# Where a two-model transformer kernel keeps its split weights and its activation rows in SBUF

## The chip, the cores and the metric

One core of one Trainium2 chip. The metric is the device time of one execution in microseconds (us); the kernel before is given as the median of three runs, and one further execution was profiled.

## The reference

Two small transformer blocks follow each other, each with two layers, on one sequence of 256 tokens with 1024 features, in float32. Layer of the first block: feed-forward, a mixing stage (latent attention, a gated recurrence, attention over a memory), feed-forward. Layer of the second block: feed-forward, a mixing stage (an RWKV-7 scan, a retention group), feed-forward. Cut to what matters here:

```python
for l in range(2):
    x = x + 0.5 * swiglu(rmsnorm(x, ffn1_norm[l]), w_ffn1_in[l], w_ffn1_out[l])   # 1024 -> 2*2816 -> 1024
    u = rmsnorm(x, mix_norm[l])
    c_q, c_kv, k_r, hq, hf, hi, hgate, mq, gate_logits = split_sizes(u @ w_in[l], IN_SPLITS)
    ...
    x = x + merged @ w_out[l]
    x = x + 0.5 * swiglu(rmsnorm(x, ffn2_norm[l]), w_ffn2_in[l], w_ffn2_out[l])
```

Nearly all the arithmetic is products of a [256, K] activation with a [K, N] weight matrix that is used once.

## The kernel before, in words

Activations lie transposed: features on the 128 partitions, the 256 tokens in the free dimension, so that one 128-feature tile of `x` is a row of 256 floats (1024 bytes) in each partition. All weights come from HBM as one stream of 128x128 blocks in the order in which they are used.

**Products in three parts.** A float32 product is made of three TensorE matmuls in the rounded type float32r: the operands are split into a high part and the remainder, and `hi*hi`, `hi*lo` and `lo*hi` are added up in PSUM. `gemm` does it for one block: the stationary operand is the block's high part (slot `sb_whi`), with the activations' high row `xh` and then their low row `xl` moving; then the block's low part (slot `sb_wlo`) with `xh` moving. Each is a 128x128 stationary operand and a 256-column moving one. There are 17,628 such matmuls. In 312 more (`gemm_rows`) the roles are changed: 128 columns of the activations are stationary and 512 columns of the weights move. The attention, recurrence and scan parts use plain float32 matmuls of several sizes.

**The weight pipeline.** SP loads a chunk of 16 blocks (1 MB) into one of three `sb_raw` slots (`load_chunk`). A piece is 8 blocks: ScalarE (ACT) copies it, rounded, into one of four `sb_whi` slots (`split_hi`), VectorE (DVE) writes the remainder to the `sb_wlo` slot of the same number (`split_lo`), and TensorE (PE) reads both (`take`). A slot is written again when PE has used its piece. `split_ahead` issues the splits up to four pieces ahead.

**The placement.** `sbuf` takes tensors one after another from the low end. The large area of temporaries, `arena`, lies at the high end, and `area` places tiles in it at fixed offsets:

```python
ctx.enter_context(nc.sbuf_tensor("arena", [128, ARENA], F32, side="right"))
k.arena, k.placed = nc.sbuf_usable_end // 32 * 32 - 4 * ARENA, 0
k.xh, k.xl = (area(k, (XH + NX * i) * T, NX, T, dt=F32R) for i in range(2))
```

Addresses are byte offsets within a partition. In the program as built the four `sb_whi` slots begin at 56480, 60576, 64672 and 68768 and the four `sb_wlo` slots at 72864, 76960, 81056 and 85152: all are 160 past a multiple of 1024, that is 32 past a multiple of 64. A block is 512 bytes, so blocks begin 160 or 672 past a multiple of 1024. The `arena` begins at 90080, and every 1024-byte row in it begins 992 past a multiple of 1024, again 32 past a multiple of 64. Rows of `xh` and `xl`, which hold the normalized input of a stage, are the moving operand in 11,712 of the 17,628 matmuls; other rows of the arena (the hidden layer of the feed-forward, the outputs of the branches) in the other 5,916.

The order of the work is written out by the Python code itself: each engine has a list of instructions and explicit semaphore waits.

Of the kernel before, what the change touches and what calls it, by code (L numbers as in the profile page):

```python
# [11 lines left out]
F32 = mybir.dt.float32  # L12
F32R = mybir.dt.float32r
# [3 lines left out]
T = 256  # L17
D = 1024
NX = 8
# [4 lines left out]
PIECE = 8  # L24
CHUNK_BLOCKS = 16
PER_CHUNK = CHUNK_BLOCKS // PIECE
WARM = 7
RAW_SLOTS = 3
SPLIT_SLOTS = 4
AHEAD1 = (2, (6, 2))  # L30
AHEAD2 = (4, (1, 1, 1, 1))
# [193 lines left out]
STATE2 = 108 * T  # L225
XH = 120
assert STATE2 + NC2 <= XH * T
ARENA = (XH + 16) * T


def constants():
# [72 lines left out]
def activation(out, a, f, **kw):  # L304

    return lambda e: e.activation(out, a, f, **kw)  # L306
# [92 lines left out]
def new_slot(k, name):  # L399

    slot = State()
    slot.sem, slot.count = k.ctx.enter_context(k.nc.semaphore(name)), 0
    return slot


def sbuf(k, name, shape, dt=F32):
    return k.ctx.enter_context(k.nc.sbuf_tensor("sb_" + name, shape, dt))


def area(k, at, *shape, dt=F32, rows=128):  # L410

    n = int(np.prod(shape))
    assert dt == U8 or at + n <= ARENA, (at, n)
    k.placed += 1
    a = k.nc.alloc_sbuf_tensor_at(f"area{k.placed}", [rows, n], dt, offset=k.arena + 4 * at)[:, :]
    if len(shape) == 1:
        return a
    names = "abcd"[:len(shape)]
    return a.rearrange(f"p ({' '.join(names)}) -> p {' '.join(names)}", **dict(zip(names, shape)))
# [26 lines left out]

def start_weights(k, stream):

    w = k.w = State()
    w.stream, w.chunks, w.pieces, w.at = stream, stream.shape[0], stream.shape[0] * PER_CHUNK, 0
    w.raw = [sbuf(k, f"raw{i}", [128, CHUNK_BLOCKS * 128]) for i in range(RAW_SLOTS)]
    w.hi = [sbuf(k, f"whi{i}", [128, PIECE * 128], F32R) for i in range(SPLIT_SLOTS)]
    w.lo = [sbuf(k, f"wlo{i}", [128, PIECE * 128], F32R) for i in range(SPLIT_SLOTS)]
    w.slots = [new_slot(k, f"raw_in{i}") for i in range(RAW_SLOTS)]
    w.loaded, w.hi_done, w.lo_done, w.used = {}, {}, {}, {}


def load_chunk(k, c):  # L460
    w = k.w
    if c >= w.chunks:
        return
    if c >= RAW_SLOTS:
        k.sp.wait(k.dve, w.lo_done[(c - RAW_SLOTS + 1) * PER_CHUNK - 1])
    n = k.sp.dma(w.slots[c % RAW_SLOTS], w.raw[c % RAW_SLOTS][:, :], w.stream[c])
    for p in range(PER_CHUNK):
        w.loaded[c * PER_CHUNK + p] = (w.slots[c % RAW_SLOTS], n)

# [10 lines left out]
def raw_piece(k, n):  # L480
    c, part = divmod(n, PER_CHUNK)
    return k.w.raw[c % RAW_SLOTS][:, part * PIECE * 128:(part + 1) * PIECE * 128]


def split_hi(k, n):
    w = k.w
    k.act.wait(*w.loaded[n])
    if n >= SPLIT_SLOTS:
        k.act.wait(k.pe, w.used[n - SPLIT_SLOTS])
    w.hi_done[n] = k.act.mark(activation(w.hi[n % SPLIT_SLOTS][:, :], raw_piece(k, n), ACT.Copy))  # L490


def split_lo(k, n):
    w = k.w
    k.dve.wait(k.act, w.hi_done[n])
    if n >= SPLIT_SLOTS:
        k.dve.wait(k.pe, w.used[n - SPLIT_SLOTS])
# [163 lines left out]
def scales(k, name, at=None):  # L661


    sc = State()
    if at is None:
        sc.ssq, sc.diag, sc.sq = (sbuf(k, f"{name}_{n}", [128, T])[:, :] for n in ("ssq", "diag", "sq"))
        sc.ms, sc.tm = (sbuf(k, f"{name}_{n}", [128, 2])[:, :] for n in ("ms", "tm"))
    else:
        sc.ssq, sc.diag, sc.sq = (area(k, at + T * i, T) for i in range(3))
        sc.ms, sc.tm = area(k, at + 3 * T, 2), area(k, at + 3 * T + 8, 2)  # L670
    sc.rs = sc.diag
    return sc
# [1047 lines left out]
def prelude2(k):  # L1720

    k.act.wait(k.pe, k.pe.count)
    k.act.wait(k.dve, k.dve.count)
    k.c2 = area(k, STATE2, NC2)
    k.c2_slot = new_slot(k, "in_c2")
    k.c2_in = k.act.dma(k.c2_slot, k.c2, k.io["c2"])
    k.lora_slot = new_slot(k, "in_lora")
# [787 lines left out]
def gains(phases):  # L2515

    names = {"f1": "ffn1_norm", "mix": "mix_norm", "f2": "ffn2_norm"}
    out = []
    for i in reversed(range(len(phases))):
        p = phases[i]  # L2520
        s = "_2" if p[0] == "B" else ""
        out.append(("final_norm" + s, None, out[-1] if out else None) if p.endswith("norm") else
                   (names[p[2:]] + s, int(p[1])))
    return out[::-1]


def warm_up(k):


    zeros = area(k, (2 * NF + 9) * T, T)  # L2530
    k.pe.wait(k.dve, k.dve.mark(memset(zeros, 0.0)))
    for i in range(WARM):
        k.pe.mark(matmul(k.bank[7][:, 0:T], zeros[:, 0:128], zeros))
# [29 lines left out]
def constants_ready(k):  # L2563

    if k.constants:
        for q in (k.pe, k.act, k.dve, k.pool):
            q.wait(*k.constants)
        k.constants = None


def store(k):
    slot = new_slot(k, "stored")
    for j in range(0, NX, 2):
        k.sp.wait(k.dve, k.x_done[j + 1])
        n = k.sp.dma(slot, k.io["out"][:, j:j + 2, :], k.x[:, j:j + 2, :])
    k.sp.wait(slot, n)


def program(nc, io, phases=PHASES):
    with ExitStack() as ctx:  # L2580
        k = State()
        k.nc, k.ctx, k.io = nc, ctx, io
        k.later, k.fillers, k.unsettled, k.units, k.emptied = deque(), deque(), None, 0, {}
        k.two, k.preloaded = None, 0
        k.sp, k.pe, k.act, k.dve, k.pool = (Queue(ctx.enter_context(nc.semaphore(f"done_{n}")))
                                            for n in ("sp", "pe", "act", "dve", "pool"))
        k.bank = [ctx.enter_context(nc.psum_tensor(f"bank{i}", [128, 512], F32)) for i in range(8)]
        k.x, k.vecs, k.c1 = sbuf(k, "x", [128, NX, T]), sbuf(k, "vecs", [128, NV]), sbuf(k, "c1", [128, NC1])
        k.sx, k.scratch = scales(k, "x"), sbuf(k, "scratch", [128, 2])[:, :]
        ctx.enter_context(nc.sbuf_tensor("arena", [128, ARENA], F32, side="right"))  # L2590
        k.arena, k.placed = nc.sbuf_usable_end // 32 * 32 - 4 * ARENA, 0
        k.xh, k.xl = (area(k, (XH + NX * i) * T, NX, T, dt=F32R) for i in range(2))
        k.x_done, k.xh_done, k.xl_done = [0] * NX, [0] * NX, [0] * NX
        g = gains(phases) + [None]
        start_weights(k, io["stream"])
        if phases[0].endswith(("f1", "f2")):
            warm_up(k)
        start(k, g[0])
        steps = []
        if any(p in ("A0mix", "A1mix") for p in phases):  # L2600
            steps = prelude1(k)
            if not phases[0].endswith(("f1", "f2")):
                constants_ready(k)
            if phases[0] not in ("A0f1", "A0f2", "A1f1"):
                for step in steps:
                    step()
                steps = []
        for i, p in enumerate(phases):
            between = {}
            if p in ("A0f1", "A0f2", "A1f1") and steps:  # L2610
                between.update({1 + j: step for j, step in enumerate(steps)})
                steps = []
            if p in ("A0f1", "A1f1") and phases[i + 1:]:
                between[14] = lambda l=int(p[1]): memory_operands(k, l)
            if p == "B0f1" or (i == 0 and p in ("B0mix", "B0f2", "B1f1", "B1mix")):
                between[2] = lambda: prelude2(k)
            if p.endswith("norm"):
                if g[i + 1] is None:
                    final(k)
            elif p in ("A0mix", "A1mix"):  # L2620
                if i == 0:
                    memory_operands(k, int(p[1]))
                mix1(k, int(p[1]), g[i + 1])
            elif p in ("B0mix", "B1mix"):
                if i == 0:
                    prelude2(k)
                mix2(k, int(p[1]), g[i + 1])
            else:
                ffn(k, g[i + 1], between, lag=i == 0)
        store(k)  # L2630
        with nc.Block() as block:
            @block.sync
            def _(e):
                k.sp.replay(e)

            @block.tensor
            def _(e):
                k.pe.replay(e)

            @block.scalar  # L2640
            def _(e):
                k.act.replay(e)

            @block.vector
            def _(e):
                k.dve.replay(e)

            @block.gpsimd
            def _(e):
                k.pool.replay(e)  # L2650
# [34 lines left out]
```

How the kernel before makes its waits and increments, by code:

```python
    def wait(self, other, count):  # L375
        if count:
            self.todo.append(lambda e: e.wait_ge(other.sem, count))
# [4 lines left out]
    def mark(self, what):  # L383
        self.count += 1
        self.todo.append(lambda e: what(e).then_inc(self.sem, 1))
        return self.count
# [1 line left out]
    def dma(self, slot, out, a):  # L388
        slot.count += 16
        self.todo.append(lambda e: e.dma_start(out, a).then_inc(slot.sem, 16))
        return slot.count
```

## Time and profile before

| | |
|---|---|
| median of three runs | 2478.52 us (2473.41 to 2479.93) |
| the profiled execution, its own time | 2470.84 us |
| its span in the profile | 2469.0 us |
| TensorE busy | 2440.9 us, 99% of the span, 20,948 matmul records |
| mean granted TensorE clock | 0.996 |
| VectorE, ScalarE, GpSimd busy | 68%, 52%, 16% |
| moved from HBM | 405.89 MB, 165 GB/s over the span |

The span runs from the first to the last instruction of the profiled execution; 1.8 us of its time lie around it. Matmuls are pipelined, and their ends are modelled: the mean duration of a record (280 ns) overlaps the next ones, and it is the distance from one start to the next that tells what a matmul takes of the engine's time. Below, that distance is called the pace.

### The profile page before, as it was taken

The numbers are of one execution on the slowest core, as the hardware profiler recorded it, in microseconds if no ns is written. First come the engines' busy times: TensorE is split into PE (matmuls) and PEld (weight loads), VectorE is DVE, ScalarE is ACT, GpSimd is POOL, SyncE is SP. The second block draws the span as 40 slices with busy tenths as digits, with TensorE's granted clock in tenths as the row PEclk, the third lists the DMA queues.
The fourth block names the chain that finished last, engine by engine and source line by source line (L and its number), as shares of the span: only waits on it lengthen the run. The fifth ranks groups of instructions, "written<-read, shape, count | busy, mean of one in ns | idle before, by whom it ended". The sixth has DMA issues, their size and how long they took to land.

```text
span 2469.0 us, 49272 instructions
## 1 busy us (share of the span) xinstructions
PE 2440.9 (99%) x20948; PEld 2380.7 (96%) x20948; DVE 1673.3 (68%) x2315; ACT 1279.0 (52%) x1812; POOL 404.8 (16%) x357
## 2 busy tenths in 40 slices
PE   8999999999999999999999999999999999999998
PEld 8999999999999999999999999989999999999998
DVE  7765776866667657878666766866666665866664
ACT  5544656644445456565454544745444444754443
POOL 4012110300200210203003013512002003422001
PEclk9999999999999999999999999999999999999999
DMA  6555433455555544345555555403555555402553
GB/s 241 188 188 180 162 124 133 173 188 186 188 188 188 188 171 154 120 139 195 185 190 191 205 203 183 155 19 120 186 185 179 187 189 186 161 26 98 193 188 120
DMA packets 57675, 410.11 MB, mean 166 GB/s; under 512 B 6384, under 2 KB 6640, under 8 KB 8688
## 3 DMA queue, kind: packets, MB, share of 16 engines
q1 hardware_dynamic: 56592, 402.15, 45.9%
q10 hardware_dynamic: 864, 4.82, 0.5%
q8 instruction: 165, 2.70, 0.4%
q14 instruction: 54, 0.44, 0.1%
HBM read 405.89 MB, written 1.05 MB: 165 GB/s over the span
## 4 chain that ended last, share of the span: by engine, by line
PE 87%; DVE 5%; ACT 3%; issue 3%; POOL 2%; DMA 0%; DVEq 0%; SPq 0%; POOLq 0%; ACTq 0%
PE bank L297 86%; DVE sb_wlo L310 2%; ACT area L306 2%; DVE area L310 2%; DVE area L321 1%; PE bank L301 1%; ACT sb_whi L306 1%; POOL area L310 0%; ACT L306 0%; POOL sb_x_ssq L310 0%; POOL area L315 0%; POOL sb_x_sq L310 0%; DVE sb_x L321 0%; DMA sb_x<-x 0%; POOL area L334 0%
## 5 line engine op out<-in xcount | busy, mean ns | idle before, releaser
L297 PE MATMUL bank<-area,sb_whi 128*128 128x256 f32 x11752 | 2093.6, 281 | 11.0 <-DVE area L321 5.7
L297 PEld LDWEIGHTS bank<-area,sb_whi 128*128 128x128 f32 x11752 | 1799.7, 188 | 23.8 <-DVE area L321 9.6
L297 PE MATMUL bank<-area,sb_wlo 128*128 128x256 f32 x5876 | 1642.3, 279 | 4.5 <-DVE sb_wlo L310 4.4
L306 ACT ACTIVATE sb_whi<-sb_raw 128x1024 fp32r<-128x1024 f32 x762 | 801.9, 1058 | 777.0 <-PE bank L297 771.0
L297 PEld LDWEIGHTS bank<-area,sb_wlo 128*128 128x128 f32 x5876 | 1103.6, 188 | 6.4 <-DVE sb_wlo L310 6.4
L310 DVE TENSOR_TENSOR sb_wlo<-sb_raw,sb_whi 128x1024 fp32r<-128x1024 f32 x762 | 962.0, 1271 | 163.2 <-ACT sb_whi L306 161.8
L310 DVE TENSOR_TENSOR area<-area,area 128x256 f32<-128x256 f32 (+7 forms) x502 | 259.7, 526 | 248.4 <-ACT area L306 245.7
L306 ACT ACTIVATE area<-area 128x256 f32<-128x256 f32 (+6 forms) x515 | 252.1, 498 | 83.9 <-DVE area L310 59.1
L310 DVE TENSOR_TENSOR area<-bank,sb_x_diag 128x512 f32<-128x512 f32 x244 | 167.3, 686 | 36.2 <-PE bank L297 21.6
L297 PE MATMUL bank<-area,area 128*64 128x64 f32 (+5 forms) x2304 | 181.4, 254 | 2.1 <-ACT area L306 1.9
L310 POOL TENSOR_TENSOR sb_x_ssq<-sb_x 128x256 f32<-128x256 f32 x12 | 13.1, 1088 | 1014.9 <-DVE sb_x L321 883.0
L297 PEld LDWEIGHTS bank<-area,area 128*64 128x64 f32 (+2 forms) x2304 | 157.8, 157 | 21.2 <-ACT area L306 7.7
L306 ACT ACTIVATE area<-bank 64x512 f32<-64x512 f32 (+5 forms) x174 | 88.0, 514 | 153.1 <-PE bank L301 112.3
L310 DVE TENSOR_TENSOR area<-bank,area 128x512 f32<-128x512 f32 (+5 forms) x204 | 105.1, 543 | 81.3 <-PE bank L297 44.2
L310 POOL TENSOR_TENSOR sb_x_sq<-sb_x 128x256 f32<-128x256 f32 x84 | 102.0, 1214 | 232.4 <-DVE sb_x L321 228.9
L321 DVE SCALAR_TENSOR_TENSOR sb_x<-bank,sb_x 128x256 f32<-128x256 f32 x96 | 39.5, 422 | 138.6 <-PE bank L297 138.6
L310 POOL TENSOR_TENSOR area<-area 128x512 f32<-128x512 f32 (+1 forms) x66 | 73.3, 1111 | 352.6 <-DVE area L310 177.6
L306 ACT ACTIVATE area<-sb_x,sb_vecs 128x256 fp32r<-128x256 f32 (+1 forms) x96 | 47.0, 506 | 76.1 <-DVE sb_x L321 73.2
L310 POOL TENSOR_TENSOR sb_x_ssq<-sb_x_ssq,sb_x_sq 128x256 f32<-128x256 f32 x87 | 79.7, 916 | 26.3 <-ACT sb_x_sq L306 19.7
L321 DVE SCALAR_TENSOR_TENSOR area<-sb_x,sb_vecs,area 128x256 fp32r<-128x256 f32 x88 | 70.3, 814 | 10.1 <-ACT area L306 10.1
L310 POOL TENSOR_TENSOR area<-area,area 128x256 f32<-128x256 f32 (+2 forms) x36 | 53.8, 1507 | 93.4 <-ACT area L306 36.0
L297 PE MATMUL bank<-sb_whi,area 128*128 128x512 f32 x208 | 66.6, 401 | 1.0 <-ACT area L306 0.6
(82 smaller groups left out, 705.7 us busy)
## 6 DMA issues: line engine op xcount, KB each, us to landing
sb_raw<-stream SPq DMA_DIRECT2D x379, 1024.0 KB, 4.8
sb_raw<-stream SPq DMA_DIRECT2D x4, 512.0 KB, 6.9
area<-lora ACTq DMA_DIRECT2D x2, 768.0 KB, 4.5
area<-c ACTq DMA_DIRECT2D x1, 1504.0 KB, 7.2
sb_x<-x SPq DMA_DIRECT2D x4, 256.0 KB, 5.0
area<-mem ACTq DMA_DIRECT2D x1, 1024.0 KB, 8.2
out<-sb_x SPq DMA_DIRECT2D x4, 256.0 KB, 2.9
area<-m ACTq DMA_DIRECT2D x1, 512.0 KB, 5.8
```

Of the source, the lines that this page charges most:

```text
L297: return lambda e: e.matmul(out, lhsT, rhs, start=start, stop=stop, skip_group_check=True, tile_position=at)
L301: return lambda e: e.transpose(out, a, ident)
L306: return lambda e: e.activation(out, a, f, **kw)
L310: return lambda e: e.tensor_tensor(out, a, b, op)
L321: return lambda e: e.scalar_tensor_tensor(out, a, s, b, op0, op1)
```

## The change

No instruction is added, removed or moved: both programs have the same instructions in the same order on every engine, with the same waits. What differs is where tiles lie.

- A new function `place` puts the arena at a multiple of 1024 bytes, and below it, from the highest down, the weight slots: slot 3, then 2, 1 and 0, in each the high part above the low part, each tile 64 * (i + 1) past a multiple of 1024. Below them lie the three raw slots.
- The rows of `xh` and `xl` are moved up by 8 floats, so that they begin 32 past a multiple of 1024. All other rows of the arena begin at a multiple of 1024.
- The scratch for descriptors of dynamic DMAs, at the low end of SBUF, goes from 16384 to 1024 bytes, which makes room for the gaps.

In the program as built:

| tile | before, past a multiple of 1024 | after |
|---|---|---|
| `sb_whi` and `sb_wlo` slots 0, 1, 2, 3 | 160, 160, 160, 160 | 64, 128, 192, 256 |
| the odd blocks in them | 672 in all | 576, 640, 704, 768 |
| rows of `xh`, `xl` | 992 | 32 |
| other 1024-byte rows of the arena | 992 | 0 |
| `sb_raw` slots | 160 | 64 |
| `sb_x`, `sb_vecs` and the constants in `sb_c1` | 128, 128, 32 | 128, 128, 32 |

```diff
+ROW = 4 * T
...
-ARENA = (XH + 16) * T
+ARENA = (XH + 16) * T + 8
...
+def place(k, end):
+    k.arena = (end - 4 * ARENA) // ROW * ROW
+    at, k.split_at = k.arena, {}
+    for i in range(SPLIT_SLOTS)[::-1]:
+        for part in range(2):
+            rest = 64 * (i + 1)
+            at = (at - 4 * PIECE * 128 - rest) // ROW * ROW + rest
+            k.split_at[part, i] = at
+    k.raw_at = []
+    for i in range(RAW_SLOTS):
+        at -= 4 * CHUNK_BLOCKS * 128
+        k.raw_at.append(at // 32 * 32)
+    return k.raw_at[-1]
...
-    w.raw = [sbuf(k, f"raw{i}", [128, CHUNK_BLOCKS * 128]) for i in range(RAW_SLOTS)]
-    w.hi = [sbuf(k, f"whi{i}", [128, PIECE * 128], F32R) for i in range(SPLIT_SLOTS)]
-    w.lo = [sbuf(k, f"wlo{i}", [128, PIECE * 128], F32R) for i in range(SPLIT_SLOTS)]
+    nc, piece, chunk = k.nc, [128, PIECE * 128], [128, CHUNK_BLOCKS * 128]
+    w.hi, w.lo = ([nc.alloc_sbuf_tensor_at(f"sb_{name}{i}", piece, F32R, offset=k.split_at[part, i])
+                   for i in range(SPLIT_SLOTS)] for part, name in enumerate(("whi", "wlo")))
+    w.raw = [nc.alloc_sbuf_tensor_at(f"sb_raw{i}", chunk, F32, offset=k.raw_at[i]) for i in range(RAW_SLOTS)]
...
-        ctx.enter_context(nc.sbuf_tensor("arena", [128, ARENA], F32, side="right"))
-        k.arena, k.placed = nc.sbuf_usable_end // 32 * 32 - 4 * ARENA, 0
-        k.xh, k.xl = (area(k, (XH + NX * i) * T, NX, T, dt=F32R) for i in range(2))
+        k.placed = 0
+        low = place(k, nc.sbuf_usable_end // 32 * 32)
+        ctx.enter_context(nc.sbuf_tensor("placed", [128, (nc.sbuf_usable_end - low) // 32 * 8], F32, side="right"))
+        k.xh, k.xl = (area(k, (XH + NX * i) * T + 8, NX, T, dt=F32R) for i in range(2))
...
-    nc = bacc.Bacc("TRN2", target_bir_lowering=False, num_devices=1)
+    nc = bacc.Bacc("TRN2", target_bir_lowering=False, num_devices=1, dynamic_dma_scratch_size=1024)
```

## Rows read from the trace of the kernel before

**Rows 1.** The page, busy time and instructions of each engine.

```profile
PE 2440.9 (99%) x20948; PEld 2380.7 (96%) x20948; DVE 1673.3 (68%) x2315; ACT 1279.0 (52%) x1812; POOL 404.8 (16%) x357
```

**Rows 2.** The page, the chain that ended last, by engine.

```profile
PE 87%; DVE 5%; ACT 3%; issue 3%; POOL 2%; DMA 0%; DVEq 0%; SPq 0%; POOLq 0%; ACTq 0%
```

**Rows 3.** The page, groups of instructions: busy, mean ns; idle before, releaser.

```profile
L297 PE MATMUL bank<-area,sb_whi 128*128 128x256 f32 x11752 | 2093.6, 281 | 11.0 <-DVE area L321 5.7
L297 PE MATMUL bank<-area,sb_wlo 128*128 128x256 f32 x5876 | 1642.3, 279 | 4.5 <-DVE sb_wlo L310 4.4
...
L306 ACT ACTIVATE sb_whi<-sb_raw 128x1024 fp32r<-128x1024 f32 x762 | 801.9, 1058 | 777.0 <-PE bank L297 771.0
...
L310 DVE TENSOR_TENSOR sb_wlo<-sb_raw,sb_whi 128x1024 fp32r<-128x1024 f32 x762 | 962.0, 1271 | 163.2 <-ACT sb_whi L306 161.8
```

**Rows 4.** Stretches of 100 us: length, busy (records), clock, DMA share, GB/s.

```profile
100.00:200.00 100.00, 100.00 (x852) 1.00 0.54 187
...
1400.00:1500.00 100.00, 100.00 (x885) 1.00 0.54 192
...
1900.00:2000.00 100.00, 100.00 (x850) 1.00 0.53 191
```

**Rows 5.** Two stretches, all engines: PE, PEld, DVE, ACT, POOL, clock, DMA.

```profile
689.00:789.00 100.00, 100.00 (x852) 100.00 (x851) 69.54 (x98) 51.01 (x78) 0.00 (x0) 1.00 0.52 182
1389.00:1489.00 100.00, 100.00 (x885) 100.00 (x884) 67.00 (x86) 49.11 (x69) 8.64 (x7) 1.00 0.54 192
```

**Rows 6.** PE's timeline at 700 us (start us, us, instruction).

```profile
700.05 0.28 PE L297 MATMUL bank<-area,sb_wlo 128*128 128x256 f32 x1
700.17 0.40 PE L297 MATMUL bank<-area,sb_whi 128*128 128x256 f32 x2
700.40 0.28 PE L297 MATMUL bank<-area,sb_wlo 128*128 128x256 f32 x1
```

**Rows 7.** PE's timeline at 1400 us.

```profile
1400.07 0.28 PE L297 MATMUL bank<-area,sb_wlo 128*128 128x256 f32 x1
1400.18 0.39 PE L297 MATMUL bank<-area,sb_whi 128*128 128x256 f32 x2
1400.41 0.28 PE L297 MATMUL bank<-area,sb_wlo 128*128 128x256 f32 x1
```

**Rows 8.** PE's timeline where one pace gives way to the other, at 1343 us.

```profile
1343.22 0.59 PE L297 MATMUL bank<-sb_x_diag,sb_c 128*128 128x256 f32 x2
1343.65 0.59 PE L297 MATMUL bank<-area,sb_c 128*128 128x256 f32 x2
```

**Rows 9.** The seven stretches with the closer pace (columns as in rows 4).

```profile
19.40:25.40 6.00, 6.00 (x55) 1.00 0.90 288
332.20:341.40 9.20, 9.20 (x77) 1.00 0.30 109
998.90:1008.10 9.20, 9.20 (x76) 1.00 0.29 105
1148.50:1152.30 3.80, 3.80 (x35) 1.00 0.44 142
1344.20:1521.40 177.20, 177.20 (x1566) 1.00 0.57 202
2155.80:2222.90 67.10, 66.67 (x1030) 1.00 0.09 33
2275.60:2277.80 2.20, 2.20 (x22) 1.00 0.92 384
```

**Rows 10.** PE's timeline in `gemm_rows`, 512 moving columns, at 220 us.

```profile
219.91 0.39 PE L297 MATMUL bank<-sb_wlo,area 128*128 128x512 f32 x1
220.14 0.63 PE L297 MATMUL bank<-sb_whi,area 128*128 128x512 f32 x2
220.61 0.39 PE L297 MATMUL bank<-sb_wlo,area 128*128 128x512 f32 x1
```

## The prediction, made before the changed kernel ran

> **What bounds the kernel now.** The page comes first. PE is busy 99% of the span and DVE, the next, 68% [rows 1]; the chain of waits that ended last lies 87% on PE [rows 2]. The groups of instructions say what PE does: 11,752 + 5,876 = 17,628 matmuls with 256 moving columns and a weight slot as stationary operand, with only 11.0 and 4.5 us of idle time before them, while ACT's 762 splits waited 771.0 us for PE [rows 3]. So the weight pipeline is ahead of PE, and the time is set by how closely PE can follow one matmul with the next.
>
> Durations of matmul records can't tell that, since the records overlap. The stretches do: between 100 and 200 us there is nothing but these matmuls, and the row counts 852 [rows 4]. A stretch also counts records that lap over its edges, about three of 280 ns at a pace of some 118; 849 starts in 100 us are 117.8 ns each. The timeline says the same: one lo-part matmul starts at 700.05, the next at 700.40, and between them lie two with the hi part; three in 0.35 us [rows 6]. At the granted clock of 1.00, the 2.4 GHz level, 256 columns at one a cycle would be 256 / 2.4 = 106.7 ns. So 11 ns of each matmul, 17,628 x 11 = some 190 us in all, are neither columns nor a wait for another engine. This is the only large thing that a change of addresses can touch.
>
> **What those 11 ns are.** Between 1400 and 1500 us the same kind of matmul runs at 885 records in 100 us [rows 4]; less three, 882 starts, 113.4 ns. The timeline there has three in 0.34 us [rows 7]. The clock is 1.00 in both stretches, DMA at 0.52 and 0.54, DVE at 69.5 and 67.0 us of 100, ACT at 51.0 and 49.1, and POOL has more work in the quicker stretch [rows 5]. So neither the clock, nor the other engines, nor the DMA traffic makes the difference of 4.4 ns. Addresses don't either, as far as this kernel varies them: in both stretches the weight blocks begin 160 or 672 past a multiple of 1024 and the rows 992 past one. What differs is how PE came into the stretch: the quicker pace begins behind the four float32 matmuls of a norm at 1343 us [rows 8] and holds from 1344.2 to 1521.4 us over 1,566 records [rows 9]. It thus looks like two streams that read side by side, the moving columns of one matmul and the weights of the next, and that get in each other's way more or less often by how they are aligned in time. Two more rows bear on it. With 512 moving columns three take 0.70 us [rows 10], 233 ns each; 512 / 2.4 is 213.3, so the excess is 20 ns, about twice that of 256 columns, though as many weights are loaded. And the two passes of a plain float32 matmul with 256 columns start at 1343.22 and end with the next start at 1343.65 [rows 8], 215 ns each, 2 x 106.7 and hardly more: where columns are taken at half the rate, there is no such excess. The cost is thus tied to moving columns that are read at the full rate, and two phases of it exist. If the phase in time decides, then so can the phase in address: 32 bytes of a moving row are 8 columns, 3.3 ns of that stream.
>
> The Trainium skill, "TensorE: Matmul & The Clock Gate", Back-to-back issue gap, gives N/2.4 + 2.5 ns for the gap of matmuls at the full clock, which would be 109.2 ns here; the trace doesn't agree, with 117.8 and 113.4.
>
> **The change part by part.** No instruction, wait or transfer is added or moved, so every term is a difference in the duration of what is there.
>
> (a) Rows of `xh` and `xl` against the weights: 11,712 matmuls. Before, rows and weight blocks both begin 32 past a multiple of 64, the difference is a multiple of 64; now the rows begin 32 past one and the blocks at one. The trace doesn't show this relation at all. From above, the gain is bounded by the 106.7 ns of the columns, 11,712 x (117.3 - 106.7) = 124 us (117.3 is the mean over both paces). From below nothing excludes a loss; the nearest row is the step between the two paces, 4.4 ns, taken the other way: 11,712 x 4.4 = 52 us lost. I take the quicker of the two paces that are seen, 113.4, since it is a state in which this kernel runs for 177 us at a time, and the slower one is held with rows and blocks in equal phase, which this change ends. About 1,850 of the 17,628 are at it already [rows 9], counted without the records at the edges and those of other forms, so 0.9 x 11,712 x 4.4 = 46 us.
>
> (b) The other moving rows, 5,916 matmuls: rows and blocks now both begin at a multiple of 64, so their difference is a multiple of 64 as before. If only the difference counts, nothing; if the start of a row counts, as much as in (a): 0.9 x 5,916 x 4.4 = 23 us. I take half, 12 us.
>
> (c) Four slots at four offsets. Within a piece the three matmuls of a block see one offset; it changes at each eighth block. It makes the result a mean over four cases, in which one bad slot would cost a quarter of (a). No term of its own.
>
> (d) The 312 matmuls with 512 columns: 20 ns excess each, 6 us at the very most; nothing is taken.
>
> (e) ACT and DVE write the slots and rows at new addresses. A split takes 1058 and 1271 ns [rows 3]; per piece of 24 matmuls PE takes 24 x 117.8 = 2.8 us, so either could become half as slow again and still be hidden. If it were not, PE would wait at the first block of a piece. Raw slots and the smaller scratch: the loads run at half of the DMA engines' time [rows 4], and all issues are from SP and ACT. Nothing.
>
> Sum: 46 + 12 = 58 us off the profiled execution's 2470.8, 2413. The median of the runs is 7.7 us above that execution; how long the quicker pace is held by chance may well make such differences, and they shrink if it is held nearly always. I add 2: **2415 us**.
>
> **The rivals.** *Addresses don't matter.* For it: within the weights, blocks at 160 and at 672 go at one pace, and the pace changes without any change of address. The Trainium skill says so as well: in "TensorE: Matmul & The Clock Gate", Step-by-step, TensorE has two independent read ports, and "Loading the next tile's weights doesn't steal SBUF read bandwidth from the running matmul". By that rule the change moves nothing; the trace shows the excess but not its cause, so it neither agrees nor disagrees. Against it: I find no other source for an excess that comes in two sizes. 160 and 672 differ by 512, so they say nothing of smaller steps. Time: 2478.5, with the lengths of the two paces drawn anew.
>
> *The new phase is a worse one.* The slower pace is the common one; a third, still slower, may exist. Place: the 11,712 matmuls of (a), or the blocks of one or two slots. Price: one more step of 4.4 ns, 117.8 to 122.2, 52 us on 2478.5: 2530. It decides the sign once the mean over the slots is over 117.3. For it: the trace shows only that starts 32 past a multiple of 64 give what we see, and nothing of rows whose phase differs from the weights'. Against it: the slower pace already has the excess at 11 of 107 ns.
>
> *The excess goes altogether.* Only if it is all collision and the new offsets avoid it for `xh` and `xl`: 124 us, 2347.
>
> **How the numbers follow.** Forecast, a quicker pace for most of the matmuls, 0.50; excess gone 0.06; no matter 0.22; worse 0.22. About 0.3% (7 us) is what a measurement of this kernel can tell from no change. So faster 0.56, same 0.22, slower 0.22. The range reaches from 2345, the excess gone for `xh` and `xl`, to 2495, which takes in no change and a small loss, and leaves out most of the worse case. The forecast's own range is 2390 to 2450: both kinds of rows at 113.4 give 2470.8 - 70 = 2401, half of (a) alone gives 2448.
>
> **What would show it.** Records in 100 us stretches of the feed-forward: 885 right, 850 for the second, 820 for the third, over 900 for the fourth. If only `xh` and `xl` count, the stretches of the first feed-forward products go to 885 and those of the second, whose moving rows are the hidden layer, stay at 850. If the slots differ, the timeline shows it every eight blocks. Busy times of ACT and DVE should stay within a few us of 1279 and 1673, and the number of records on every engine the same. The prediction is wrong if both paces appear in the same places as before, or if the pace is above 118 anywhere.

## The result, and the profile after

The changed kernel takes 2488.18 us, median of five runs (2486.91 to 2491.09), against 2478.52 us of the kernel before (2473.41 to 2480.99, five runs). The ratio is 1.0045, with a 95% interval of 1.003 to 1.0059: slower by about 10 us, where 2415 us and a gain were forecast. The profiled execution took 2488.18 us with a span of 2486.3 us, 17.3 us over the 2469.0 us of the profiled execution before. That one was quicker than all five runs before, so the distance between the profiles is larger than that between the medians.

The page after, engines and the groups that answer to [rows 1, 3]:

```profile
PE 2459.4 (99%) x20948; PEld 2400.4 (97%) x20948; DVE 1675.1 (67%) x2315; ACT 1279.0 (51%) x1812; POOL 405.0 (16%) x357
...
L298 PE MATMUL bank<-area,sb_whi 128*128 128x256 f32 x11752 | 2112.5, 283 | 10.8 <-DVE area L322 5.0
...
L298 PE MATMUL bank<-area,sb_wlo 128*128 128x256 f32 x5876 | 1653.2, 281 | 3.5 <-DVE sb_wlo L311 3.5
L307 ACT ACTIVATE sb_whi<-sb_raw 128x1024 fp32r<-128x1024 f32 x762 | 801.6, 1057 | 792.7 <-PE bank L298 785.7
...
L311 DVE TENSOR_TENSOR sb_wlo<-sb_raw,sb_whi 128x1024 fp32r<-128x1024 f32 x762 | 961.7, 1270 | 170.1 <-ACT sb_whi L307 168.8
```

The same instructions in the same numbers. ACT and DVE take as long as before for a split (1057 and 1270 ns, before 1058 and 1271), PE idles no more ahead of its matmuls, and ACT waits 785.7 us for PE where it waited 771.0. The work of the other engines stood still; what moved is PE's own pace.

Stretches of 100 us of the kernel after (length, PE busy and records, granted clock, DMA share, GB/s), which answer to [rows 4]:

```profile
100.00:200.00 100.00, 100.00 (x851) 1.00 0.55 189
500.00:600.00 100.00, 100.00 (x846) 1.00 0.52 187
...
1400.00:1500.00 100.00, 100.00 (x847) 1.00 0.51 186
1900.00:2000.00 100.00, 100.00 (x846) 1.00 0.50 180
```

846 or 847 records in three of the four, where the wider pace of before gives 850 to 852, and no stretch with 885. The timeline shows that this is a mean over very different things. In the feed-forward's second product the moving row is the hidden layer, at a multiple of 1024. At 155 us PE reads weight slot 0, 8 us later slot 3 (start us, us, instruction):

```profile
154.65 0.28 PE L298 MATMUL bank<-area,sb_wlo 128*128 128x256 f32 x1
...
154.99 0.28 PE L298 MATMUL bank<-area,sb_wlo 128*128 128x256 f32 x1
...
155.33 0.28 PE L298 MATMUL bank<-area,sb_wlo 128*128 128x256 f32 x1
```

```profile
163.07 0.28 PE L298 MATMUL bank<-area,sb_wlo 128*128 128x256 f32 x1
163.20 0.41 PE L298 MATMUL bank<-area,sb_whi 128*128 128x256 f32 x2
163.44 0.28 PE L298 MATMUL bank<-area,sb_wlo 128*128 128x256 f32 x1
...
163.80 0.28 PE L298 MATMUL bank<-area,sb_wlo 128*128 128x256 f32 x1
```

Three matmuls take 0.34 us with the weights 64 bytes past the row's place, and 0.365 us (the mean of the two distances shown) with the weights 256 past it. The order of the instructions says which slot each matmul reads; matched with the trace's start times, it gives the mean pace of each kind of moving row against each slot. (Here and below: the distance to the next start, for matmuls of 256 columns that follow each other, without those over 130 ns.)

| | slot 0 | slot 1 | slot 2 | slot 3 |
|---|---|---|---|---|
| before, rows at 992, all slots at 160 | 117.3 | 117.4 | 117.3 | 117.3 |
| after, `xh` and `xl` at 32; slots at 64, 128, 192, 256 | 118.4 | 118.7 | 119.7 | 116.8 |
| after, other rows at 0 | 116.3 | 118.5 | 117.7 | 119.8 |

So addresses do count, by more than 3 ns of 118, and in the mean they count against the change: 118.30 ns against 117.31. Over some 17,360 such distances that is 17.2 us, all but 0.1 of the 17.3 us between the spans. In the sums below the same time is split in two: 17 more distances of the changed kernel lie over 130 ns (197 against 180), so that the sum up to 130 ns grows by 15.1 us (2053.2 against 2038.1) and the sum of the longer ones by 2.0 (62.4 against 60.4). All else on PE is 0.1 us apart (363.1 against 363.0).

### The profile page after: what moved, and what is told of

The parts are those of the page before. It is cut to its first block, busy times and chain, and to the rows that moved or that the text cites. A ratio compares the mean times of both kernels' runs of the same rounds, so it can differ in the third digit from the quotient of the medians.

```text
span 2486.3 us, 49272 instructions
## 1 busy us (share of the span) xinstructions
PE 2459.4 (99%) x20948; PEld 2400.4 (97%) x20948; DVE 1675.1 (67%) x2315; ACT 1279.0 (51%) x1812; POOL 405.0 (16%) x357
## 4 chain that ended last, share of the span: by engine, by line
PE 88%; DVE 5%; ACT 3%; issue 3%; POOL 1%; DMA 0%; DVEq 0%; POOLq 0%; SPq 0%; ACTq 0%
PE bank L298 87%; DVE sb_wlo L311 2%; ACT area L307 2%; DVE area L311 2%; DVE area L322 1%; PE bank L302 1%; ACT sb_whi L307 1%; ACT L307 0%; POOL sb_x_ssq L311 0%; POOL area L311 0%; DVE sb_x L322 0%; POOL sb_x_sq L311 0%; DMA sb_raw<-stream 0%; DVE area L317 0%; DVE sb_x L311 0%
## 5 line engine op out<-in xcount | busy, mean ns | idle before, releaser
L307 ACT ACTIVATE sb_whi<-sb_raw 128x1024 fp32r<-128x1024 f32 x762 | 801.6, 1057 | 792.7 <-PE bank L298 785.7
L311 DVE TENSOR_TENSOR sb_wlo<-sb_raw,sb_whi 128x1024 fp32r<-128x1024 f32 x762 | 961.7, 1270 | 170.1 <-ACT sb_whi L307 168.8
L322 DVE SCALAR_TENSOR_TENSOR area<-sb_x,sb_vecs,area 128x256 fp32r<-128x256 f32 x88 | 70.2, 813 | 9.7 <-ACT area L307 9.7
```

The lines of the kernel that those rows point to most:

```text
L311: return lambda e: e.tensor_tensor(out, a, b, op)
L322: return lambda e: e.scalar_tensor_tensor(out, a, s, b, op0, op1)
```

## The experiments

Three theories are told apart, A, B and C, as the first expectation states them; A is the one held. In all of the kernels the instructions, their order and their waits are those of the two kernels; only places differ. "Difference" is where a weight block begins, less where the moving row begins, in bytes; blocks lie 512 apart and rows 1024, so that it is given within 512. In the edits shown here the numbers stand where the kernels read them from a table of their own.

**u192 and u64: one difference for all matmuls.** Rows all at a multiple of 1024, all eight slots at 192, or at 64.

```diff
-            rest = 64 * (i + 1)
+            rest = 192    # u192; 64 in u64
...
-        k.xh, k.xl = (area(k, (XH + NX * i) * T + 8, NX, T, dt=F32R) for i in range(2))
+        k.xh, k.xl = (area(k, (XH + NX * i) * T, NX, T, dt=F32R) for i in range(2))
```

> All rows of activations begin at a multiple of 1024, all eight weight slots 192 past one: the same difference (192) as in the kernel before, the whole moved by 32 bytes. Theory A, only the difference between weight block and moving row counts (modulo 512): the two paces of before, 117.8 and 113.4 ns, nothing else, and a time within 0.3% of the kernel before, 2471 to 2486 us. Theory B, the start of a row or block at a multiple of 64 counts by itself: one pace that before does not have, 1% or more away from it. Theory C, the offset that changes every eight blocks is what costs in the changed kernel, whatever the offsets: as A here.

> Rows at a multiple of 1024, all slots 64 past one (difference 64). In the changed kernel the blocks of slot 0 against rows at a multiple of 1024 have this difference, and there three matmuls take 340 ns in many places and 353 in the others. Theory A: those two paces, with more of the closer one than before: between 2402 us (113.4 ns nearly everywhere) and 2478 us. Theory B: as u192, since both kernels begin rows and blocks at multiples of 64. Theory C: the kernel before, 2478 us.

Measured: u192 2479.03 us, ratio to the kernel before 1.0027 (1.0018 to 1.0037). u64 2424.25 us, 0.98 (0.9783 to 0.9816). u192 has one of the two paces of before, three in 353.3 ns, in all but some ten blocks: the difference of before, shifted as a whole by 32 bytes, gives its wider pace, and the closer one, which the kernel before held in one matmul of ten, is not entered. That makes 7.7 us in the spans' sums (2045.8 us against 2038.1). u64 is at the closer pace, 113.3 ns, in 67% of the distances, with a mean of 114.8. Stretches of 100 us, of u192 and then of u64 (columns as above):

```profile
500.00:600.00 100.00, 100.00 (x851) 1.00 0.52 189
```

```profile
500.00:600.00 100.00, 100.00 (x885) 1.00 0.55 199
1900.00:2000.00 100.00, 100.00 (x885) 1.00 0.52 186
```

B falls for the values of the paces: both kernels start all rows and blocks at multiples of 64 and are 2% apart. C falls too: it put both at the time of before, as both have one offset throughout.

**probe_a, probe_b, probe_c, probe_d: four differences in one kernel.** Rows at a multiple of 1024, a value for each slot. For steps under 32 bytes the slot's tensor is made longer and the weights begin some floats into it.

```diff
-            rest = 64 * (i + 1)
+            rest = (0, 32, 96, 160)[i]    # probe_a; (224, 320, 384, 448)[i] in probe_b; 32 in probe_c and probe_d
...
+SHIFT = (4, 6, 10, 12)    # probe_c; (7, 9, 11, 20) in probe_d
...
-    nc, piece, chunk = k.nc, [128, PIECE * 128], [128, CHUNK_BLOCKS * 128]
+    nc, piece, chunk = k.nc, [128, PIECE * 128 + 64], [128, CHUNK_BLOCKS * 128]
...
+                   [:, SHIFT[i]:SHIFT[i] + PIECE * 128]
```

> Rows at a multiple of 1024, slots 0 to 3 at 0, 32, 96 and 160 past one: four differences in one kernel, read from the starts of the matmuls piece by piece. Theory A: each slot has paces of its own, between 113 and 122 ns, and slot by slot the same in each feed-forward. Theory C: all four slots alike, at 118 ns. Theory B: slots 1, 2 and 3 (32 past a multiple of 64) alike and different from slot 0.

> As probe_a with slots at 224, 320, 384 and 448. Theory A: paces of their own again; slot 2 (384) and slot 3 (448) are 192 + 192 and 64 + 384, and tell whether the pattern repeats at less than 512 bytes: if it repeats at 128, slot 1 (320), slot 3 (448) go like 64, with 113 ns in places, and slot 2 like 0. Theory C: all alike at 118 ns.

> Slots at 48, 56, 72 and 80 past a multiple of 1024, rows at one: differences around the 64 that gave the closer pace. If reads are taken in units of 64 bytes or so, a step of 8 or 16 bytes changes little and all four slots have the 340 ns of three matmuls in many places; if the match must be exact to a few bytes, none has it, and all lie at 117 to 120 ns, near 2485 us.

> Slots at 60, 68, 76 and 112: the same question with steps of 4 bytes. Coarse units: slots 0 to 2 at 113 to 118 ns like u64, slot 3 like the 118.8 ns of difference 96 or the 118.5 of 128. Exact match needed: slots 0 to 2 over 117 ns.

One run each: 2503.70, 2476.04, 2487.43 and 2487.29 us. Paces in ns, with what the other kernels give for the same difference:

| difference | 0 | 32 | 48 | 56 | 60 | 64 | 68 | 72 | 76 | 80 |
|---|---|---|---|---|---|---|---|---|---|---|
| ns | 119.8 | 118.3 | 118.1 | 117.9 | 119.3 | (see text) | 118.4 | 118.4 | 116.4 | 118.7 |

| difference | 96 | 112 | 160 | 224 | 320 | 384 | 448 |
|---|---|---|---|---|---|---|---|
| ns | 118.8 | 119.6 | 119.7 | 117.8 | 116.1 | 118.5 | 117.8 |

(For 60 the bound is set at 160 ns, since a quarter of its blocks hold a distance over 130.) Theory A stands for the paces: they follow the difference. As far as four pairs show, they repeat at 256: 384 has the 118.5 of 128, 448 the 117.8 of 192, 320 the 116.1 next to 115.8 of 64 (rows_back, below), 256 in the changed kernel the 119.8 of 0. The guess in probe_b of a repeat at 128 is wrong, as 384 would have had to go like 0. Of the two guesses on fine steps neither is right: 60 and 68 have nothing of the closer pace of 64, and 76 has it again. In probe_d the blocks of the slot at 76 take three matmuls in 340 ns, or in 360, whole pieces at a time.

**arena_down: the kernel before with its arena 128 bytes lower.**

```diff
-        ctx.enter_context(nc.sbuf_tensor("arena", [128, ARENA], F32, side="right"))
-        k.arena, k.placed = nc.sbuf_usable_end // 32 * 32 - 4 * ARENA, 0
+        ctx.enter_context(nc.sbuf_tensor("arena", [128, ARENA + 32], F32, side="right"))
+        k.arena, k.placed = nc.sbuf_usable_end // 32 * 32 - 4 * ARENA - 128, 0
```

> The kernel before, with nothing changed but the arena, and so every activation row, 128 bytes lower: rows 864 past a multiple of 1024, slots at 160 as before, difference 320, which is 64 past a multiple of 256. Rows and blocks both begin 32 past a multiple of 64, as before. Theory A (only the difference counts, and repeats at 256, as the two probes say): as u64, both paces with 113.4 ns for well over half of the matmuls, 2415 to 2440 us. Theory B (starts at multiples of 64 are what gave u64 its gain): 2478 us, the kernel before.

Measured: 2465.01 us, ratio 0.998 (0.997 to 0.999). The two paces are those expected, 340 and 353.3 ns for three, but the closer one is held in 28% of the distances only, and the time is outside both expectations.

**all_up32: u64 with the arena and all slots 32 bytes higher.**

```diff
-    k.arena = (end - 4 * ARENA) // ROW * ROW
+    k.arena = (end - 4 * ARENA) // ROW * ROW + 32
...
+            rest = 96    # u64: 64
```

> u64 with everything 32 bytes higher: all rows of the arena 32 past a multiple of 1024, all slots 96 past one, difference 64 again. arena_down left open why its closer pace held for 28% of the matmuls and that of u64 for 61%: its difference is 320, not 64, and its rows begin 32 past a multiple of 64. If the start against 64 is what lowered the share: about 2465 us here. If the 256 between 64 and 320: 2424 us. In both cases the two paces are 113.3 and 117.8 ns.

Measured: 2466.85 us, ratio 0.9973 (0.9961 to 0.9985), the closer pace in 25%. Values as in u64, share as in arena_down. (For u64 the expectation says 61%; counted over all distances it is 67%.) Here theory A ends: a difference fixes which paces exist, but two kernels with the same difference are 1.8% apart. The timeline of u64 shows the places where the pace is decided:

```profile
206.81 0.28 PE L299 MATMUL bank<-area,sb_wlo 128*128 128x256 f32 x1
206.92 0.39 PE L299 MATMUL bank<-area,sb_whi 128*128 128x256 f32 x2
207.15 0.28 PE L299 MATMUL bank<-area,sb_wlo 128*128 128x256 f32 x1
207.26 0.50 PE L299 MATMUL bank<-sb_c,sb_x_ssq 128*128 128x2 f32 x4
207.62 0.48 PE L299 MATMUL bank<-area,sb_whi 128*128 128x256 f32 x2
207.94 0.28 PE L299 MATMUL bank<-area,sb_wlo 128*128 128x256 f32 x1
208.06 0.40 PE L299 MATMUL bank<-area,sb_whi 128*128 128x256 f32 x2
208.29 0.28 PE L299 MATMUL bank<-area,sb_wlo 128*128 128x256 f32 x1
```

Three in 0.34 us ahead of a norm's four small matmuls, three in 0.35 behind them. The same in stretches of 100 us of all_up32; in arena_down it is the one from 1400 us that has 885:

```profile
100.00:200.00 100.00, 100.00 (x885) 1.00 0.52 191
500.00:600.00 100.00, 100.00 (x852) 1.00 0.53 190
```

The starts in the traces tell more of it, in one profiled execution of each. Each kernel has 85 to 91 series of at least twelve 256-column matmuls without another kind or a wait between them, and but for its edges a series keeps one pace. The closer pace is held in 45 of 88 in u64, in 49 of 89 in all_up32 and in 52 of 87 in arena_down, so in about half in all three, but in 7 of 85 before and 1 of 85 in u192. Eight of the series are long, with 1,151 to 1,559 matmuls, 12,016 of the 17,628 together. Of these eight, six have the closer pace in u64, one in all_up32, one in arena_down. Five such series more (7,747 matmuls, 4.4 ns each, 34 us) are the 31.0 us between the spans of u64 and all_up32, with a little given back by short ones. So in these executions the start against 64 does not lower the number of series that take the closer pace; what differs is which ones do. Each layout repeats its time (u64 2420.7 to 2435.8 us in four runs, all_up32 2464.4 to 2470.2 in ten, no overlap), so the choice is not drawn wholly anew at each execution. Whether the start steers it or a small difference in time ahead of each series does stays open.

**rows_back and slots_same: the change with one of its parts undone.**

```diff
-        k.xh, k.xl = (area(k, (XH + NX * i) * T + 8, NX, T, dt=F32R) for i in range(2))
+        k.xh, k.xl = (area(k, (XH + NX * i) * T, NX, T, dt=F32R) for i in range(2))    # rows_back
...
-            rest = 64 * (i + 1)
+            rest = 64    # slots_same
```

> The changed kernel with one part undone: rows of xh and xl at a multiple of 1024 like the other rows, slots at 64, 128, 192, 256. Every matmul has one of the differences 64, 128, 192, 256. Theory A: all pieces go as those against rows at 0 go in the changed kernel: slots 0 to 3 at 116.4, 118.5, 117.7, 119.8 ns, mean 118.1, so 17,400 x 0.2 = 3 us less than the changed kernel, about 2485 us. The rival (the 32 bytes of xh and xl are what costs): back to the 117.3 ns of before, 2470 to 2480 us.

> The other part of the change undone: all slots at 64, rows of xh and xl left at 32 past a multiple of 1024, the others at one. Differences 32 for xh and xl, 64 for the others. Theory A: 118.3 ns for xh and xl (slot 0 of the changed kernel has 118.4), 114.8 for the others as in u64; 11,700 x 1.0 more and 5,900 x 2.5 less than the mean of before, so about the time of before, 2465 to 2475 us. If the slots at four offsets made the whole loss: as u64, 2424 us.

Measured: rows_back 2483.06 us, 5 less than the changed kernel, with 115.8, 118.5, 117.8 and 119.9 ns for its slots: as theory A has it, and the rival falls. slots_same 2481.47 us, over the 2465 to 2475 expected. `xh` and `xl` are at 118.3 as expected; the others, at difference 64, are at 116.5 instead of 114.8, again the share of the closer pace. So either part undone gives back 5 to 7 us, in one run each, and both undone (u64) 64. With difference 64 in all matmuls the closer pace is held in 67% of the distances; here, where only the other rows have it, in about 30% of their blocks. all_up32, with 25% at difference 64 throughout, shows that the same difference everywhere is not enough for a high share.

**u76 and u0: the best and the worst difference in all slots.**

```diff
-SHIFT = (4, 6, 10, 12)
+SHIFT = (11, 11, 11, 11)    # u76, from probe_c
...
-            rest = 64 * (i + 1)
+            rest = 0    # u0, from the changed kernel with all rows at a multiple of 1024
```

> All slots 76 past a multiple of 1024, rows at one. In probe_d the slot at 76 was at 340 ns for three matmuls in over half of its blocks and at 360 in nearly all others. Uniform, the kernel stays in whichever it enters: 2400 us if the closer pace wins everywhere, 2510 if the wider one does, a share of each in between. If neighbouring slots made those paces, another value altogether.

> Weight slots and rows all at a multiple of 1024, difference 0, as someone would lay them out who aligns everything. probe_a had 360 ns for three matmuls in 1,144 of 1,405 blocks of slot 0. Theory A: 119.9 ns throughout, 17,400 x 2.6 = 45 us more than before, about 2518 us. If it was the alternation of slots: 2478 us.

Measured: u76 2419.56 us (2419.00 to 2419.86), ratio 0.9776 (0.975 to 0.9802). u0 2512.28 us, one run. Stretches of 100 us of u76, then of u0 (columns as above):

```profile
500.00:600.00 100.00, 100.00 (x884) 1.00 0.54 194
...
1900.00:2000.00 100.00, 100.00 (x885) 1.00 0.53 193
```

```profile
500.00:600.00 100.00, 100.00 (x833) 1.00 0.50 184
...
1900.00:2000.00 100.00, 100.00 (x835) 1.00 0.51 184
```

And the timeline of each at 1900 us:

```profile
1900.09 0.28 PE L300 MATMUL bank<-area,sb_wlo 128*128 128x256 f32 x1
1900.20 0.39 PE L300 MATMUL bank<-area,sb_whi 128*128 128x256 f32 x2
1900.43 0.28 PE L300 MATMUL bank<-area,sb_wlo 128*128 128x256 f32 x1
```

```profile
1900.22 0.28 PE L299 MATMUL bank<-area,sb_wlo 128*128 128x256 f32 x1
1900.34 0.40 PE L299 MATMUL bank<-area,sb_whi 128*128 128x256 f32 x2
1900.58 0.28 PE L299 MATMUL bank<-area,sb_wlo 128*128 128x256 f32 x1
```

0.34 us for three and 0.36, at a clock of 1.00 in both. u76 holds the closer pace in 94% of the distances, mean 113.7, and u0 stays at 120.0. A sum over PE's distances tells what becomes of it, in us:

| | 256-column matmuls up to 130 ns apart | mean ns | those further apart | all else on PE | span |
|---|---|---|---|---|---|
| before | 2038.1 | 117.31 | 60.4 | 363.0 | 2469.0 |
| after | 2053.2 | 118.30 | 62.4 | 363.1 | 2486.3 |
| u64 | 1992.2 | 114.80 | 70.2 | 363.7 | 2433.9 |
| u76 | 1968.1 | 113.74 | 79.9 | 362.2 | 2417.7 |
| u0 | 2083.5 | 119.95 | 58.3 | 361.1 | 2510.5 |

The first column and the span go together. u76 is 70.0 us down there, and 19.5 come back as longer distances. About 8 us of both figures have only changed the column, since 70 more distances lie over 130 ns (250 against 180). The pace itself gives 62 us (17,303 distances, 117.31 - 113.74 ns) and 11 are lost again, which is why u76 misses 2400. About 6.5 of the 11 lie in stretches with a lower clock: the mean granted clock is 0.993, where the kernel before has 0.996, with seven stretches at the 1.2 GHz level before the end, the kernel before three. The rest are waits, which grew a little, from

```profile
PE bank L297 <- DVE area L321: 5.7, 9, 2.0
PE bank L297 <- DVE sb_wlo L310: 4.8, 9, 0.9
PE bank L297 <- ACT area L306: 3.6, 8, 0.6
PE bank L297 <- DVE area L310: 3.5, 3, 3.0
```

to, in u76 (who waited for whom: us in all, times, longest),

```profile
PE bank L300 <- DVE area L324: 6.3, 7, 2.0
PE bank L300 <- DVE sb_wlo L313: 6.3, 5, 1.9
PE bank L300 <- DVE area L313: 5.0, 4, 3.7
PE bank L300 <- ACT area L309: 4.4, 10, 0.7
```

which is 4.4 us. With PE quicker, it waits no more often for ACT and DVE (26 times against 29 in these rows), but longer. u76 and u64 are the two versions that are 2% quicker than the kernel before, with ratios whose intervals overlap; arena_down and all_up32 beat it by 0.2 and 0.3%.

## Why the prediction was wrong

**What bounds the kernel: right.** PE's pace sets the time. Across five kernels with equal instructions the spans run from 2417.7 to 2510.5 us, and the sum of the close distances moves with them.

**The 11 ns as something that addresses can touch: right, and the rival "addresses don't matter" is refuted** by u0 and u76, 93 us apart with nothing but places changed. The Trainium skill says in "TensorE: Matmul & The Clock Gate", Step-by-step, that loading the next weights takes nothing from the running matmul. Taken to mean that their places are free, these runs don't agree, with 2512.28 and 2419.56 us. That it is the two reads that meet is argued from the dependence on their difference, and no run shows the event itself.

The prediction also sets the 109.2 ns of the Trainium skill ("TensorE: Matmul & The Clock Gate", Back-to-back issue gap) against the trace. It leaves out that the page gives this formula for an isolated matmul, and other figures for a stream that loads weights each time, so 117.8 ns doesn't contradict it. Nothing in the forecast rests on that comparison.

**(a) is the step that failed.** It put `xh` and `xl` at 113.4 ns, "since it is a state in which this kernel runs for 177 us at a time". They came to 118.4 in the mean of the four slots, 1.1 over the 117.3 of before. Two errors lie in it. The first is that the paces seen before, 113.4 and 117.8, were taken for all that exist, when they are the two of one difference, 192; other differences have others, and at 32, 96 and 160 the mean is 118.3 to 119.7. The second is that leaving the equal phase modulo 64 was taken for a way out of the collision. The good differences are 64 and 76, the first of them in equal phase, and 60 and 68 are bad.

**(b)** took 12 us for the other rows, half of a full change of pace. They came to 118.1 in the mean of the slots, 0.8 over before: 5 us lost.

**(c)**, "no term of its own", with one bad slot costing a quarter: the frame was right, and the slots do average. It should have been read on: four unlike values are a poor bet on all being good, and six of the eight turned out worse than the 117.3 of before. The means run from 116.3 to 119.8, and only slot 0 against rows at 0 reaches 113.3 in more than a few blocks.

**(d) and (e)** hold. The split times moved by 1 ns, and all of PE's other work by 0.1 us.

**The rival "the new phase is a worse one"** is what happened, in the place it named. Its price was too high: a mean of 1.0 ns, where one full step of 4.4 was taken. 17.2 us of the 17.3 between the profiled executions are it. Its point of decision, a mean over 117.3, was the right one, and so was one of the signs named beforehand, a pace above 118 anywhere. The time, 2488.18, lies within 2345 to 2495 only because the range was drawn to take in a small loss; that says nothing for the mechanism of (a). What was wrong is the sign, and with it the likeliest case.

## What to carry to other kernels

Where an engine is bound by back-to-back matmuls that load new weights each time, compare the distance between starts with columns over the clock; if it is some per cent over, try the place of the weights against the place of the moving rows, one offset for all slots at a time. The layout with rows and slots all at a multiple of 1024 was the worst here (2512 us, one run), and one number in it (the weights 64 or 76 bytes on) was worth 3.5%, 2% against the kernel before. Measure the layout itself: 32 bytes more on the arena and all slots cost most of that gain again (2466.85 us). Several offsets in one kernel are a good probe and a poor layout: they show the values, and average them.

## What was not expected of the hardware

- In kernels with one difference throughout, matmuls with 256 columns in float32r follow each other at 113.3, 117.8 or 120.0 ns at the full clock, according to where the weights begin against the moving row; the pattern repeats at 256 bytes in the four pairs tried. Steps of 4 to 8 bytes matter: 64 and 76 can reach 113.3 ns, 60, 68, 72 and 80 don't (117.9 to 119.3 with 56 among them).
- One difference can have two steady paces: 113.3 and 117.8 ns at 64, 113.3 and 120.0 at 76. A kernel stays in one over 1,500 matmuls and may change to the other at any other kind of matmul or wait. At 76 the closer one is held in 80 of 91 series when all slots have it, at 64 and 320 in about half, at 192 in 7 of 85 or fewer.
- 224 gave 117.8 ns with rows at a multiple of 64 and 116.8 with rows 32 past one, in kernels whose other slots differed too. Whether the start by itself or the neighbours did it was not tried.
